# One PSUM bank for both column blocks of a 256-token unit, and both halves of the weights two units ahead split ahead of emptying it

## The reference: two transformer stacks in a row

```python
# first stack, layers 0 and 1, D = 1024
u = h @ w_in                     # q, kv, conv gates, state-space inputs
y = concat(attention, short_conv, ssd) @ w_out
x = x + gate * rms_norm(y)
f = square(relu(h @ w_ff1)) @ w_ff2       # D_FF = 4096
x = x + gate2 * rms_norm(f)

# second stack, layer 0 (mixer A): three dilated groups of 16 heads of 64
q, k, v = split(x @ a_w_in)      # for each group g = 0, 1, 2
q, k = rope(q), rope(k)
o = merge(banded_attention(q, k, v))
h = (o * silu(z)) @ a_w_out
x = layer_norm(ALPHA * x + h)
x = x + sigmoid(x @ ple_w_gate) * (p @ ple_w_proj)
# second stack, layer 1 (mixer B): 16 query heads, 2 key heads, window 128, the same tail
```

## Time and profile before

| | us |
|---|---|
| median of 3 runs (1853.01 to 1865.01) | 1861.16 |
| the profiled execution, its own time | 1855.55 |
| its span in the trace | 1853.3 |
| PE busy | 1648.4 |
| DVE busy | 1062.3 |
| ACT busy | 929.2 |
| POOL busy | 105.4 |

### The profile page before, as it was taken

One profiled execution on the slowest core, in us unless ns is written; L12 is line 12 of the kernel. 1 busy time (PEld: TensorE's weight loads), 2 busy tenths in 40 slices (PEclk: granted clock), 3 DMA queues, 4 the chain that ended last, 5 costly groups with the idle time before them and its releaser, 6 DMA issues.

```text
span 1853.3 us, 26621 instructions
## 1 busy us (share of the span) xinstructions
PE 1648.4 (89%) x10291; PEld 1388.9 (75%) x10291; DVE 1062.3 (57%) x1967; ACT 929.2 (50%) x1668; POOL 105.4 (6%) x114
## 2 busy tenths in 40 slices
PE   6899888869999999779997699989999999798787
PEld 3577566637888888547665599989899998797676
DVE  1563546675343434575636776678566674576655
ACT  4353545434232313245545455558677785477635
POOL 3100023020000000020012100000000000000000
PEclk8799978888999999889987899999999999998889
DMA  8422445302323333212455256555442432342221
GB/s 291 136 68 69 159 159 180 112 28 85 120 91 92 97 107 97 70 49 67 130 161 186 91 162 201 187 178 181 144 159 92 160 121 85 114 137 76 84 69 69
DMA packets 221567, 225.45 MB, mean 122 GB/s; under 512 B 6155, under 2 KB 219985, under 8 KB 221393
## 3 DMA queue, kind: packets, MB, share of 16 engines
q1 hardware_dynamic: 220736, 223.63, 37.6%
q0 software_dynamic: 704, 0.12, 0.0%
HBM read 222.68 MB, written 1.05 MB: 121 GB/s over the span
## 4 chain that ended last, share of the span: by engine, by line
PE 71%; ACT 12%; DVE 11%; issue 3%; DMA 2%; POOL 0%; SPq 0%; DVEq 0%; ACTq 0%; POOLq 0%
PE bank L795 18%; PE bank L796 17%; PE bank L797 17%; ACT whi L1245 2%; ACT AP L1599 2%; PE bank L820 1%; ACT SH L1360 1%; PE bank L1023 1%; DVE XT L1999 1%; PE bank L866 1%; PE bank L864 1%; PE bank L865 1%; DMA raw<-in_w_mod_dram 1%; DVE AP L2221 1%; DVE wlo L1729 1%
## 5 line engine op out<-in xcount | busy, mean ns | idle before, releaser
L1729 DVE TENSOR_TENSOR wlo<-raw,whi 128x1024 fp32r<-128x1024 f32 (+3 forms) x322 | 389.5, 1210 | 326.6 <-ACT whi L1245 322.7
L1245 ACT ACTIVATE whi<-raw 128x1024 fp32r<-128x1024 f32 (+3 forms) x322 | 337.3, 1047 | 361.4 <-PE bank L797 329.1
L795 PE MATMUL bank<-HH,whi 128*128 128x512 f32 (+3 forms) x656 | 254.5, 388 | 34.6 <-DVE HL L1751 29.5
L796 PE MATMUL bank<-HL,whi 128*128 128x512 f32 (+3 forms) x656 | 250.5, 382 | 0.0
L797 PE MATMUL bank<-HH,wlo 128*128 128x512 f32 (+3 forms) x656 | 250.3, 382 | 0.0
L795 PE MATMUL bank<-HA,whi 128*128 128x256 f32 x576 | 166.8, 290 | 14.8 <-DVE LA L1751 7.4
L795 PEld LDWEIGHTS bank<-HH,whi 128*128 128x128 f32 (+2 forms) x656 | 123.3, 188 | 68.9 <-issue 23.6
L796 PE MATMUL bank<-LA,whi 128*128 128x256 f32 x576 | 163.7, 284 | 0.0
L797 PE MATMUL bank<-HA,wlo 128*128 128x256 f32 x576 | 163.6, 284 | 0.0
L797 PEld LDWEIGHTS bank<-HH,wlo 128*128 128x128 f32 (+2 forms) x656 | 123.7, 188 | 26.8 <-issue 1.0
L796 PEld LDWEIGHTS bank<-HL,whi 128*128 128x128 f32 (+2 forms) x656 | 123.9, 189 | 25.5 <-issue 1.5
(11 more groups left out here) (342 smaller groups left out, 3494.0 us busy)
## 6 DMA issues: line engine op xcount, KB each, us to landing
raw<-in_w_ff_dram SPq DMA_DIRECT2D x64, 1024.0 KB, 5.3
raw<-in_w_mod_dram SPq DMA_DIRECT2D x48, 1024.0 KB, 5.2
raw<-in_a_w_in_dram SPq DMA_DIRECT2D x40, 1024.0 KB, 5.0
raw<-in_w_in_dram SPq DMA_DIRECT2D x16, 1024.0 KB, 5.2
raw<-in_b_w_in_dram SPq DMA_DIRECT2D x9, 1024.0 KB, 5.2
raw<-in_w_out_dram SPq DMA_DIRECT2D x8, 1024.0 KB, 5.1
raw<-in_ple_w_gate_dram SPq DMA_DIRECT2D x8, 1024.0 KB, 5.2
raw<-in_a_w_out_dram SPq DMA_DIRECT2D x4, 1024.0 KB, 5.1
```

Source lines behind the costliest of these rows:

```text
L795: nc.tensor.matmul(o, wh, xh, start=start, stop=False)
L796: nc.tensor.matmul(o, wh, xl, start=False, stop=False)
L1245: f(whi[h % HALF_SLOTS][:, 0:n], raw[u.id % RAW_SLOTS][:, (h % 2) * n:(h % 2) * n + n], ACT.Copy)\
L1729: v.tensor_tensor(wlo[h % HALF_SLOTS][:, 0:n], raw[u.id % RAW_SLOTS][:, (h % 2) * n:(h % 2) * n + n], whi[h % HALF_SLOTS][:, 0:n].bitcast( ...
```

## The change: packed units, wide emptying, and the second half of unit u+2 moved forward

A unit is now **packed** if it has two blocks of 128 columns, covers 256 tokens, and is neither `mod` nor `bkv`. Both its blocks go to one bank of 512 columns, block 0 in columns 0 to 255 and block 1 in 256 to 511. Only the first matmul of block 0 starts the bank's accumulation group. One signal for both blocks comes at the unit's end. Each emptying instruction then handles both blocks at once: where there were two of 256 columns there is one of 512. `proj` units put two blocks in a bank as well. SH and RR become twice as wide; APT moves to memory that other tables have left by then.

`halves_ahead` grows by one for packed units, so the step of unit u splits both halves of unit u+2 ahead of emptying unit u. Number and order of the matmuls and of the transfers stay as they are.

```diff
+        self.packed = (blocks is not None and kind not in ("mod", "bkv") and [m for _, m in blocks] == [P, P]
+                       and all(b - a == SEQ for a, b in t))
...
-        u.halves_ahead = u.halves_next + sum(v.id == u.id + 2 for v in split_units)
+        u.halves_ahead = u.halves_next + (2 if u.packed else 1) * sum(v.id == u.id + 2 for v in split_units)
...
@@ PE, unit
+                        if u.packed and bi == 0:
+                            both = next_bank((u.id, 0), *block_readers(u, 0), *block_readers(u, 1))
+                            bank_of[(u.id, 1)] = bank_of[(u.id, 0)]
+                            open_[0], open_[1] = both[:, 0:SEQ], both[:, SEQ:T]
+                        elif u.packed:
+                            pass
...
-                        first, final = k == 0, k == KC - 1
+                        first, final = k == 0 and not (u.packed and bi == 1), k == KC - 1
...
-                    if half == 1:
+                    if half == 1 and not u.packed:
                         keys.append(("blk", u.id, bi))
+                    elif half == 1 and bi == 1:
+                        keys += [("blk", u.id, 0), ("blk", u.id, 1)]
...
@@ ACT, unit: ff1, then aq, ak and bkv
+                f(R32[i % 2], b, ACT.Relu).then_inc(*s_relu.tick(u.key))
+                act.wait_ge(s_relu, s_relu.at(u.key))
+                f(FX[:, 2 * i:2 * i + 2, :], both(R32[i % 2]), ACT.Square).then_inc(*s_fh.tick((l, g, 2 * i), (l, g, 2 * i + 1)))
...
+                for q in range(4):
+                    o = q ^ 1
+                    ins = f(SH[sh_turn[0] % 2][32 * q:32 * q + 32, 0:n, :], b[32 * o:32 * o + 32, 0:n, :], ACT.Copy)
+                ins.then_inc(*s_sh2.tick(key))
...
@@ ACT, unit: proj
-                for n in range(4):
-                    if n == 2:
+                for n in range(2):
+                    if n == 1:
                         splits(u.halves_next)
-                    m = 4 * part + n
-                    f(PJ[:, m, :], bank(u, n)[:, 0:SEQ], ACT.Copy).then_inc(*s_pj.tick((i, m)))
+                    m = 2 * part + n
+                    f(PJ[:, 2 * m:2 * m + 2, :], both(bank(u, n)), ACT.Copy).then_inc(*s_pj.tick((i, m)))
...
@@ DVE, unit: aq, ak and bkv
+                v.tensor_tensor(rr, b, cos, ALU.mult).then_inc(*s_cos2.tick(key))
+                v.tensor_tensor(sh, sh, sin, ALU.mult).then_inc(*s_sin2.tick(n))
...
+                    v.tensor_tensor(dst[:, g, :, :], rr, sh, ALU.add)\
+                        .then_inc(*s_rope2.tick(key + (0,), key + (1,), ("n", n)))
```

More of the change, by code:

```diff
@@ L357, in build @@
     rope = place("rope_sb", [P, 2, SEQ])
+    APT = at("APT", [P, 1152], where["at"])
     axial = place("axial_sb", [P, 2, SEQ])
@@ L863, in unit @@
                             o = b[:, 0:256]
-                            nc.tensor.matmul(o, xh[:, k, ts_], whi[s][:, w], start=first, stop=False)
-                            nc.tensor.matmul(o, xh[:, k, ts_], wlo[s][:, w], start=False, stop=False)
-                            ins = nc.tensor.matmul(o, xl[:, k, ts_], whi[s][:, w], start=False, stop=final)
+                            ins = mm3(o, xh[:, k, ts_], xl[:, k, ts_], whi[s][:, w], wlo[s][:, w], first, final, True)
                         elif token_major:
@@ L1296, in unit @@
                     return
+                if u.packed:
+                    ps = both(bank(u, 1))
+                    keys = (u.key + (0,), u.key + (1,))
+                    if part in ("z0", "z1"):
+                        f(ZS[:, 2 * int(part[1]):2 * int(part[1]) + 2, SEQ:T], ps, ACT.Silu).then_inc(*s_u_out.tick(*keys))
+                    else:
+                        f({"q": QC, "gc": GC, "gb": GB}[part][:, :, SEQ:T], ps, ACT.Copy).then_inc(*s_u_out.tick(*keys))
+                    return
                 for bi, (c0, m) in enumerate(u.blocks):
@@ L1375, in unit @@
                     act.wait_ge(s_o2, s_o2.at((i, 4 * (hq - 2) + 3)))
-                for bi in (0, 1):
-                    f(AV[hq % 2][:, g, bi, :], bank(u, bi)[:, 0:256], ACT.Copy).then_inc(*s_v2.tick(u.key + (bi,)))
+                f(AV[hq % 2][:, g, :, :], both(bank(u, 1)), ACT.Copy).then_inc(*s_v2.tick(u.key + (0,), u.key + (1,)))
             elif kind == "az":
@@ L1693, in _ @@
                 act.wait_ge(s_ln_total, s_ln_total.at((i, "mean")))
-                f(SH[0], banks[7][:, 0:SEQ], ACT.Copy, scale=1.0 / D).then_inc(*s_ln_stat.tick((i, "mean")))
+                f(SH[0][:, 0, :], banks[7][:, 0:SEQ], ACT.Copy, scale=1.0 / D).then_inc(*s_ln_stat.tick((i, "mean")))
                 for k in range(KC):
@@ L1779, in unit @@
                 l, part = u.key
-                if part == "val":
+                if part == "val" and u.packed:
+                    b = bank(u, 1)
+                    dve.wait_ge(s_u_out, s_u_out.at((l, "gc", 1)))
+                    dve.wait_ge(s_pads, s_pads.at(l))
+                    v.tensor_tensor(TP[:, :, 1, 1:257], both(b), GC[:, :, SEQ:T], ALU.mult).then_inc(*s_val.tick((l, "val", 0), (l, "val", 1)))
+                elif part == "val":
                     for bi in (0, 1):
@@ new lines, in unit @@
+                n = sh_turn[0]
+                m = 2 if kind != "bkv" else 1
+                b = both(bank(u, m - 1))[:, 0:m, :]
+                key = u.key + ((kind,) if kind != "bkv" else ("kb",))
+                i, hq, g = (1, 0, 0) if kind == "bkv" else u.key
+                cos, sin = (bc(rope[:, w:w + 1, :], [P, m, SEQ]) for w in (0, 1))
+                sh, rr = SH[n % 2][:, 0:m, :], RR[n % 2][:, 0:m, :]
+                dve.wait_ge(s_sh2, s_sh2.at(key))
+                v.tensor_tensor(rr, b, cos, ALU.mult).then_inc(*s_cos2.tick(key))
@@ L1861, in unit @@
+                sh_turn[0] += 1
             elif kind == "out2":
                 i, j = u.key
+                v.scalar_tensor_tensor(out=V32[:, 2 * j:2 * j + 2, :], in0=XT[:, 2 * j:2 * j + 2, SEQ:T], scalar=ALPHA, in1=both(bank(u, 1)),
+                                       op0=ALU.mult, op1=ALU.add).then_inc(*s_v32.tick(u.key + (0,), u.key + (1,)))
                 for bi in (0, 1):
                     m = 2 * j + bi
-                    v.scalar_tensor_tensor(out=V32[:, m, :], in0=XT[:, m, SEQ:T], scalar=ALPHA, in1=bank(u, bi)[:, 0:SEQ],
-                                           op0=ALU.mult, op1=ALU.add).then_inc(*s_v32.tick(u.key + (bi,)))
```

184 lines of the change are left out of this document (95 added, 89 removed).

## The result

| | before | after |
|---|---|---|
| median, us (runs) | 1858.01 (4) | 1901.02 (4) |
| profiled execution: own time | 1855.55 | 1900.63 |
| its span | 1853.3 | 1898.5 |

What follows compares the result with a forecast made beforehand. Bound: the chain of waits, 71% PE. Mixer A +18.9, mixer B +7.3, tails +9.4, gains -10.1 make +25.5; with the clock's +17, +42.5 on 1861.16 gives about 1904 us, range 1868 to 1928.

Steps and rivals of the forecast that it cites:

- The chain to YA: Mixer A, steps behind aq and ak units: YA at 6.35 us against 4.65, ten stalls of 1.7, net +15 us.
- rival (e): Splits don't really move, only packing is left; ten mixer A stalls of 0.6 without a fall: about 1858, chance 0.05.
- The clock: Mixer A: 3.4 us at half speed behind each of ten stalls, 1.7 us each, +17; nothing added for mixer B.
- (a): Same stalls, longer falls of the clock, as behind the 1.27 us stall: +35 in place of +17, 1922; chance 0.12.
- (b): Same stalls, no fall of the clock: 1861.2 + 25.5, 1887; chance 0.22.
- The 1.32 us row: Profile before: a 1.32 us stall with clock 0.57 for 4 us, 3.4 us at the low level; basis for +17.
- The other waits: First AP wait +2.6, last av unit +1.3, AQ in mixer B +3.1, tails' sums +5.2, FXL 0.7 four times, +2.8.
- Mixer B: Head 0's scores +3.1, three later aq units +1.0 each, three later az units +0.4 each: together +7.3 us.
- +1.0 each: Mixer B, the other three aq units: +0.9 for later SH, less 0.7 for SH, plus 0.8 for rope, at AP.
- The gains: Waits for PJ and gate banks shrink or go, -8.2; small waits on wlo and banks go, -1.9: -10.1 us.
- Small waits on wlo and on banks that go: -1.9: Part of the gains: small waits on wlo and on banks disappear at five places, -1.9 us.
- one block can't start early, +0.7 each: Ends of the two gate phases: one block can't start early, +0.7 each, +1.4 us.

Runs made afterwards that it cites:

- the kernel with work in place of the stalls: Changed kernel plus 15 extra matmuls of 256 columns on PE at the ten mixer A steps, between scores and transposes: 1889.99 us, ratio 1.0145.
- the kernel with YA ahead by itself: Kernel before, with YA of the oldest head ahead of the rope at all steps behind aq and ak units, nothing else: 1859.01 us, ratio 0.9992.
- the kernel with the second half behind the emptying: Changed kernel, but the second half of unit u+2 is split behind the emptying of unit u on ACT and DVE: 1895.9 us, ratio 1.0174.
- the kernel with one gate unit changed: Changed kernel, but the last gate unit ahead of mixer B splits only one half of unit u+2 ahead: 1900.88 us, ratio 1.0235.

## Why the prediction was right, and where its parts were off

**The chain to YA: right.** Ten stalls of 1.68 us were measured, ten of 1.7 had been put down, and SH in four instructions takes 2.39. What was worked out link by link (the end's signal, whi, four SH, three wide rope instructions, YA) is what the timeline shows. The packing alone gives 0.67 at each of the ten, where rival (e) had 0.6.

**The clock: right in kind and number, a little large in size.** Ten falls of 3.4 us were forecast, ten were found. The term was +17 at 1.7 us each; by the kernel with work in place of the stalls it is 15.4. Rivals (a) and (b) are both out for mixer A. The 1.32 us row came nearest, but that was a choice and not a finding: the rows show one fall of each length, not the three falls that rival (a) counts, and the prediction itself names two stalls without one. Against the rule of long idle gaps in the Trainium skill ("TensorE: Matmul & The Clock Gate", section "HAM oscillation — how this bites in real kernels") stand ten falls behind stalls of 1.68 us; for its account of short idle spells between groups of matmuls ("A second HAM failure mode: psum-queue depth-cycling") stands that the falls are gone when the idle time is filled, though the ten spells of 0.67 us in the packing alone have none.

**The other waits: right.** First AP wait 3.84 (forecast 3.9); the last `av` unit's 1.9 where 0.6 grows by 1.3; AQ in mixer B 3.2 (3.1); ACC 13.6 less 8.6, +5.0 for two places (5.2), the longest now 4.70 against 2.06 and 2.6; FXL 0.5 four times, 2.1 (2.8).

**Mixer B: right in size, but at another wait, and with terms that were left out.** The "+1.0 each" for the three later `aq` units was put at AP, where PE stood 2.53 us before and stands 2.53 now. It came ahead of P times V, where PE waits for YA; the kernel before, then the changed one:

```profile
1689.25 0.67 PE L1132 MATMUL bank<-APT,AV 128*128 128x256 f32 x2 [0.46 <-DVE YA L2246]
```

```profile
1732.68 0.67 PE L1145 MATMUL bank<-APT,AV 128*128 128x256 f32 x2 [1.49 <-DVE YA L2294]
1736.10 0.90 PE L1124 MATMUL bank<-ident_sb,AP 128*128 128x128 f32 x3 [2.53 <-DVE AP L2282]
```

The three waits for YA are 1.0, 1.0 and 1.4 us longer, and the AP waits between them 0.0, 0.4 and 0.4 (0.4 each forecast). Not forecast were a first AP wait that is 1.5 shorter (0.58 for 2.08), one of 1.75 for APT at 1805.48, and 6.8 us more at the low clock (47.8 against 41.0), for which the prediction put nothing. So that 4.7 + 3.2 = 7.9 us came out so near 7.3 is partly luck.

**The gains: right where listed, and one missing.** The waits for PJ and for the gate unit's bank went. But the first `wout` unit of layer 1 gave 2.8 us more: its block 1 stood 4.09 us in the kernel before for a bank that ACT's mod_row holds, and packed it asks for no second bank. What holds it then is 1.25 us:

```profile
1019.31 0.36 PE L804 MATMUL bank<-HX,whi 128*128 128x256 f32 x1 [1.25 <-DVE HXL L1779]
```

From 1000 to 1034 of the kernel before every packed kernel here is 3.6 to 4.5 us shorter, and the two that are not packed are not. The other 2.3 of layer 1's 6.6 us prove nothing: from 791 to 1000 the kernel with YA ahead by itself, whose program there is that of the kernel before, is 2.2 shorter too. The step that failed is "Small waits on wlo and on banks that go: -1.9".

**The end of the first gate phase: wrong.** The step was "one block can't start early, +0.7 each". It counted one late block, and not that ACT comes late into the phase and can't catch up. In the changed kernel ACT begins the Sigmoid of the first gate unit at 1664.04, 4.0 us behind that unit's end. From then on ACT and DVE, with two splits a unit ahead of the chain Sigmoid, RR, XT, YH, need 5.73 us for a unit, and PE 5.4 to 5.7:

```profile
1674.69 0.60 ACT L1425 ACTIVATE SH<-bank 128x512 f32<-128x512 f32 x1
1677.71 0.63 ACT L1429 ACTIVATE YH<-XT 128x512 fp32r<-128x512 f32 x1 [2.42 <-DVE XT L1937]
1678.37 2.00 ACT L1258 ACTIVATE whi<-raw 128x1024 fp32r<-128x1024 f32 x2
1680.41 0.60 ACT L1425 ACTIVATE SH<-bank 128x512 f32<-128x512 f32 x1
```

The last Sigmoid still comes 3.4 us behind its unit's end, at 1677.0. With one split a unit ACT starts 3.2 us late and is 0.2 late at the last. The `bkv` unit, which asks for three banks at once, stands 2.72 us for that bank, with a low clock of 17.1 us behind, for which the prediction put nothing ("For mixer B I add nothing"). That made the start of mixer B 14.3 us longer where 0.7 + 3.1 were meant.

So the sum was hit partly by misses of opposite sign: about +10 at that place (14.3 against 3.8), and on the other side about -5 in layer 1, about half of it no effect of the change, and -4 in mixer A's first wait and steps (30.7 against 2.6 + 15 + 17 = 34.6). The likeliest story was the right one, and mixer A's part of it is 30.7 of the 45.1 us between the two profiled executions; that the total agrees within a microsecond is luck.

## What to carry to other kernels

Before moving work ahead in an engine's order, list what stands behind it up to the instruction that the critical engine asks for, and on every engine of that chain: in the changed kernel 1.1 us of whi cost 43, and putting it behind the emptying moved 1.2 us of wlo into the same place. If that instruction doesn't need the work ahead of it, move it first: YA ahead of the rope took off 27 us here, and turned a packing worth 0.35% by itself into the fastest kernel (1842.0). Price a stall of PE with the fall of the clock behind it, here 1.7 and 1.5 us, and count banks and engine time per unit over several units, since a lateness that an engine never catches up shows only at the unit that asks for more.

## What the runs showed of the hardware

The clock fell behind every one of the ten stalls of 1.68 us in the changed kernel, behind nine of ten of 1.8 to 2.1 in the kernel with the second half behind the emptying, and behind none of the ten of 0.67 in the packing alone. A longer stall isn't always followed by a fall: behind the 2.80 us at 1633.29 and the 2.08 at 1670.67 the kernel before kept a clock of 1.00, up to 1679.9. How long it stayed low doesn't follow from the stall either. At the one wait for SH of the `bkv` unit, with the same work of PE behind it, it was 3.4 us behind 2.31, 17.1 behind 2.72, and 6.8 behind 2.86, 3.26 and 3.82.

At a granted clock of 1.00 matmuls of 256 columns don't always come at one pace. The feed-forward part has 885 in 100 us before; the kernel with one gate unit changed, whose program there is the changed kernel's, has this row:

```profile
1100.00:1200.00 100.00, 99.20 (x847) 98.80 (x846) 60.18 (x60) 47.51 (x52) 0.00 (x0) 1.00 0.59 187
```

That is one per 0.117 us against 0.113, 3.7% slower with hardly a wait and a clock that reads full; the changed kernel has 871 in the same window. In one and the same execution both paces occur. The feed-forward part of that kernel is 5.8 us longer than the changed kernel's, most of it for the pace and some 1.4 for 2.8 us more at the low level. What sets the pace isn't shown. Such stretches and the falls in layer 0, whose code no kernel here touches (from 116 to 137 us at the low level), are large enough to hide a few us at one place in a median of this kernel.
